# Rotary query halves exchanged by transfers between SBUF places, and the rotary tile copied out by ScalarE

## The reference, cut to what matters

```python
cq = rms_norm(h @ w_dq, q_gain)
q = jnp.einsum('bsr,rhd->bshd', cq, w_uq)          # 16 heads, 128 plain + 64 rotary dimensions
q = jnp.concatenate([q[..., :NOPE_DIM], rope(q[..., NOPE_DIM:], pos)], axis=-1)
q = rms_norm(q, qk_gain_q) * qk_gain_k.astype(q.dtype)

def rope(x, pos):                                   # cos, sin of pos * inv, half = 32
    x1, x2 = x[..., :half], x[..., half:]
    return jnp.concatenate([x1 * cos - x2 * sin, x1 * sin + x2 * cos], axis=-1)
```

## Time and profile before

| what | value |
|---|---|
| runs | 2076.65, 2082.14, 2082.95 us, median 2082.14 |
| the profiled execution | 2079.32 us, span 2077.6 us |
| TensorE busy | 2054.7 us, 99% of the span |
| VectorE busy | 1601.5 us, 77% |
| ScalarE busy | 1104.7 us, 53% |
| GpSimd busy | 342.0 us, 16% |
| granted TensorE clock | 1.000 |

### The profile page before, as it was taken

The page is one execution under the profiler, slowest core; times in us unless marked ns, Lnnn a source line. Parts: engine busy times, 40 slices in busy tenths (PEclk is TensorE's granted clock), DMA queues, the critical chain, the costliest instruction groups (busy, mean ns, idle before and its releaser), DMA issues.

```text
span 2077.6 us, 44241 instructions
## 1 busy us (share of the span) xinstructions
PE 2054.7 (99%) x16692; PEld 1990.6 (96%) x16692; DVE 1601.5 (77%) x2667; ACT 1104.7 (53%) x1898; POOL 342.0 (16%) x384
## 2 busy tenths in 40 slices
PE   9999999999999999999999999999999999999999
PEld 8999999999999999999999999998768889999998
DVE  7779885336367998987999898679665468989987
ACT  6456454443225655655665655545564446656555
POOL 0011111221011111110211111111122121111111
PEclk9999999999999999999999999999999999999999
DMA  5467783322224777775777777441322226777775
GB/s 173 116 165 181 183 194 102 99 84 83 82 82 113 178 183 187 179 183 151 163 184 183 185 174 192 132 122 30 94 72 82 62 62 158 182 187 179 187 177 129
DMA packets 362556, 293.57 MB, mean 141 GB/s; under 512 B 21592, under 2 KB 329093, under 8 KB 362149
## 3 DMA queue, kind: packets, MB, share of 16 engines
q1 hardware_dynamic: 326266, 226.84, 36.4%
q0 software_dynamic: 35824, 64.37, 19.0%
q10 hardware_dynamic: 314, 0.37, 0.1%
HBM read 224.57 MB, written 2.66 MB: 109 GB/s over the span
## 4 chain that ended last, share of the span: by engine, by line
PE 88%; DMA 5%; DVE 4%; issue 2%; ACT 1%; SPq 1%; ACTq 0%; DVEq 0%
PE side L825 28%; PE main L776 26%; PE main L825 20%; PE side L1368 2%; DMA raw<-raw 2%; PE main L1130 2%; DMA sums_w<-raw 1%; PE main L1298 1%; PE side L1338 1%; DVE w_lo L2102 1%; DMA raw<-in_ffn_w_gate 1%; PE side L1220 1%; PE main L1200 1%; PE side L1044 1%; PE main L1377 1%
## 5 line engine op out<-in xcount | busy, mean ns | idle before, releaser
L825 PE MATMUL side<-xw_hi,w_hi 128*128 128x260 f32 x1344 | 380.7, 283 | 6.0 <-ACT main L1543 2.6
L825 PE MATMUL side<-xw_hi,w_lo 128*128 128x260 f32 x1344 | 381.0, 283 | 0.0
L825 PE MATMUL side<-xw_lo,w_hi 128*128 128x260 f32 x1344 | 380.1, 283 | 0.0
L2102 DVE TENSOR_TENSOR w_lo<-raw,w_hi 128x512 fp32r<-128x512 f32 (+2 forms) x472 | 323.3, 685 | 35.1 <-ACT w_hi L1488 15.5
L825 PE MATMUL main<-xw_hi,w_hi 128*128 128x260 f32 x1008 | 286.1, 284 | 0.0
L825 PE MATMUL main<-xw_lo,w_hi 128*128 128x260 f32 x1008 | 284.7, 282 | 0.0
L825 PE MATMUL main<-xw_hi,w_lo 128*128 128x260 f32 x1008 | 284.5, 282 | 0.0
L825 PEld LDWEIGHTS side<-xw_hi,w_hi 128*128 128x128 f32 x1344 | 253.2, 188 | 8.6 <-ACT main L1543 3.5
L825 PEld LDWEIGHTS side<-xw_hi,w_lo 128*128 128x128 f32 x1344 | 253.2, 188 | 0.0
L825 PEld LDWEIGHTS side<-xw_lo,w_hi 128*128 128x128 f32 x1344 | 252.8, 188 | 0.0
L2102 DVE TENSOR_TENSOR w_lo<-sums_w,w_hi 128x1024 fp32r<-128x1024 f32 (+1 forms) x232 | 218.6, 942 | 1.0 <-ACT w_hi L1471 1.0
(11 more groups left out here) (460 smaller groups left out, 5334.4 us busy)
## 6 DMA issues: line engine op xcount, KB each, us to landing
sums_w<-raw POOLq DMA_DIRECT2D x112, 256.0 KB, 3.3
raw<-raw POOLq DMA_DIRECT2D x112, 256.0 KB, 5.1
raw<-in_ffn_w_gate SPq DMA_DIRECT2D x86, 256.0 KB, 4.4
raw<-in_ffn_w_gate SPq DMA_DIRECT2D x43, 512.0 KB, 6.1
raw<-in_ffn_w_up SPq DMA_DIRECT2D x84, 256.0 KB, 4.2
raw<-in_ffn_w_up SPq DMA_DIRECT2D x42, 512.0 KB, 6.1
raw<-in_gmlp_w_in SPq DMA_DIRECT2D x16, 1024.0 KB, 5.5
raw<-in_ffn_w_down SPq DMA_DIRECT2D x56, 256.0 KB, 3.9
```

The source lines that it names most:

```text
L825: mm = nc.tensor.matmul(into[j], w_tiles(w, weights_at(s, j))[:, k, :], moving[:, k, order[j], :], start=(j in (0, 1) and k == 0 and i == ...
L2102: a = nc.vector.tensor_tensor(dst, src, hi.bitcast(F32), ALU.subtract)
```

## The change

The eight products with the constant `swap` are left out. Instead SP issues, for each pair of heads, four transfers from `tq` to a new tile `tq_swapped`, each moving 32 partitions of 2080 bytes to the neighbouring block. The rotary tile is copied out of PSUM by ScalarE, ahead of its square, and no longer by VectorE, and has a semaphore of its own, `tq_copied`; `evac_done` counts plain tiles alone (16 in the stage). VectorE's `rope_b` reads `tq_swapped`, and stands one tile later (at u % 3 == 1); that of the last pair stands behind the copies of the turned rows. In SP's queue the exchange of pair 0 stands between page loads 20 and 21, ahead of chunk 2; that of pair 1 ahead of chunk 3; those of pairs 2 to 7 ahead of the last page loads. `tq_swapped` has one place, so an exchange waits for the `rope_b` before it. The semaphore `c_squared` is replaced by a third count on `cq_squared`.

```diff
--- before.py
+++ after.py
@@ -272,6 +272,7 @@
         cq = sb("cq", [P, 2, TOK], F32, proj)
         trig_g = sb("trig_g", [P, 2, TOK], F32, proj)
         tq = cq
+        tq_swapped = sb("tq_swapped", [P, TOK], F32, proj)
         rope_a = sb("rope_a", [P, TOK], F32, proj)
         rope_b = sb("rope_b", [P, TOK], F32, proj)
         sq_hi = sb("sq_hi", [P, 2, TOK], F32R, proj)
@@ -384,7 +385,7 @@
         factors_set = sem("factors_set")
         cq_squared = sem("cq_squared")
         cqn_set = sem("cqn_set")
-        c_squared = sem("c_squared")
+        tq_copied = sem("tq_copied")
         c_set = sem("c_set")
         kr_swapped = sem("kr_swapped")
         kr_part = sem("kr_part")
@@ -477,9 +478,14 @@
         at_ffn[2] = ffn_past(at_ffn[1])
         at_mla = ffn_past(at_ffn[2])
         at_uq = at_mla.past(chunk=2, tile=4, evac=4, h=2, rms=3)
-        at_wo = at_uq.past(chunk=4, tile=24, evac=24)
+        at_wo = at_uq.past(chunk=4, tile=24, evac=H)
         at_ffn[3] = at_wo.past(chunk=8, tile=16, evac=16, h=H, norm=1, sums=KD, xg=KD, xh=KD)
         at_ffn[3].groups = LAST_GROUPS
+
+        def nope_tiles(u):
+
+            return 2 * (u // 3) + min(u % 3, 1) + 1
+
         P_AT = [0, 1, 3, 6]
         PT_AT = [0, 4, 8, 7]
         at_end = ffn_past(at_ffn[3], last=True)
@@ -692,12 +698,26 @@
                         sp.dma_start(pieces[k][:, j, :], cache_mla[0, bass.ds(page, 1), :, :].rearrange("a p d -> (a p) d"))\
                             .then_inc(nat_in[k // 4], 16)
 
+            def swap_halves(r_):
+
+                sp.wait_ge(tq_copied, r_ + 1)
+                if r_ >= 1:
+                    sp.wait_ge(rope_b_set, r_ + 1)
+                for lo in range(0, P, ROPE // 2):
+                    other = lo ^ ROPE // 2
+                    sp.dma_start(tq_swapped[lo:lo + ROPE // 2, :], tq[other:other + ROPE // 2, r_ % 2, :])\
+                        .then_inc(swapped, 16)
+
             n = at_uq.chunk
             for c in range(4):
                 if c == 2:
                     sp.wait_ge(pages_in, 16)
                     sp.wait_ge(tile_done, at_mla.tile)
-                    load_pages(0, 6)
+                    load_pages(0, 5)
+                    swap_halves(0)
+                    load_pages(5, 6)
+                elif c == 3:
+                    swap_halves(1)
                 sp.wait_ge(lo_done, at_uq.lo + c - 1)
 
                 src = mla_w_uq[0].rearrange("(k p) h d -> k p h d", p=P)[:, :, 4 * c:4 * c + 4, :]
@@ -707,6 +727,8 @@
                         .then_inc(uq_rope_in[c % 2], 16)
                     sp.dma_start(dst[:, 0:4 * NOPE].rearrange("p (h d) -> p h d", h=4), src[k, :, :, 0:NOPE])\
                         .then_inc(uq_rope_in[c % 2] if k else raw_in[c % 2], 16)
+            for r_ in range(2, H // 2):
+                swap_halves(r_)
             sp.wait_ge(tile_done, at_wo.tile)
             sp.wait_ge(lo_done, at_wo.lo)
             load_pages(6, 10)
@@ -1078,7 +1100,7 @@
             pe.wait_ge(lo_done, n + 2)
             out_tile(0, 1, KD, xg_hi, xg_lo, free=e + 1, before={4: latent_sum})
             out_tile(1, 1, KD, xg_hi, xg_lo, free=e + 2)
-            pe.wait_ge(c_squared, 1)
+            pe.wait_ge(cq_squared, 3)
             wide_sum(2, ones, [square[:, 0, :]]).then_inc(rms_mm, 1)
             pe.wait_ge(evac_done, e + 4)
             pe.wait_ge(root_done, at_mla.rms + 2)
@@ -1087,13 +1109,6 @@
 
             n, e = at_uq.lo, at_uq.evac
             pe.wait_ge(h_lo_done, at_uq.h)
-
-            def turn_rope(u):
-
-                r_ = u // 3
-                pe.wait_ge(rope_b_set, r_ + 1)
-                pe.wait_ge(evac_done, e + u + 1)
-                wide_sum(0, swap, [tq[:, r_ % 2, :]]).then_inc(swapped, 1)
 
             def q_norms(u):
 
@@ -1120,7 +1135,12 @@
                 c, part = u // 6, u % 6
                 if part == 0:
                     pe.wait_ge(lo_done, n + c + 1)
-                pe.wait_ge(evac_done, e + u - 1)
+                if u < 2:
+                    pe.wait_ge(evac_done, e + u - 1)
+                elif u % 3 == 1:
+                    pe.wait_ge(tq_copied, u // 3)
+                else:
+                    pe.wait_ge(evac_done, e + nope_tiles(u - 2))
                 h0 = 2 * (part // 3)
                 for k in range(2):
                     for i, (w, moving) in enumerate(((w_hi, h_hi), (w_hi, h_lo), (w_lo, h_hi))):
@@ -1131,11 +1151,8 @@
                                                   moving[:, k, half * HALF:(half + 1) * HALF],
                                                   start=(k == 0 and i == 0), stop=(k == 1 and i == 2))
                 mm.then_inc(tile_done, 1)
-                if u % 3 == 0 and u > 0:
-                    turn_rope(u - 1)
                 if u >= 2:
                     q_norms(u - 2)
-            turn_rope(23)
             q_norms(22)
             q_norms(23)
             for j in range(4):
@@ -1148,8 +1165,9 @@
             mm.then_inc(kn_done, 1)
 
 
-            pe.wait_ge(rope_b_set, 9)
+            pe.wait_ge(rope_b_set, 1)
             pe.wait_ge(evac_done, at_wo.evac)
+            pe.wait_ge(tq_copied, H // 2)
             for b in range(QB + 1):
                 w = P if b < QB else NS
                 if b == 0:
@@ -1911,7 +1929,7 @@
                 act.wait_ge(cqn_set, m + 1)
                 nc.scalar.activation(h_hi[:, m, :], cq[:, m, :], ACT.Copy).then_inc(h_hi_done, 1)
             act.wait_ge(evac_done, e + 3)
-            nc.scalar.activation(square[:, 0, :], c_t[:], ACT.Square).then_inc(c_squared, 1)
+            nc.scalar.activation(square[:, 0, :], c_t[:], ACT.Square).then_inc(cq_squared, 1)
             act.wait_ge(rms_mm, at_mla.rms + 3)
             act.wait_ge(rstd_done, at_mla.rms + 2)
             nc.scalar.activation(halves(root[:, :]), side[:, 2:4, 0:HALF], ACT.Sqrt, scale=1.0 / KL,
@@ -1925,8 +1943,18 @@
                     act.wait_ge(q_ssq, u - 1)
                 elif u >= 2:
                     act.wait_ge(sq_lo_set, 2 * ((u - 2) // 3) + (u - 2) % 3 + 1)
-                act.wait_ge(evac_done, e + u + 1)
-                src = tq[:, u // 3 % 2, :] if part % 3 == 2 else qn[:, 4 * c + 2 * (part // 3) + part % 3, :]
+                if part % 3 == 2:
+                    src = tq[:, u // 3 % 2, :]
+                    if u >= 6:
+                        act.wait_ge(tq_squared, u - 5)
+                        act.wait_ge(rope_a_set, u // 3 - 1)
+                        act.wait_ge(swapped, 64 * (u // 3 - 1))
+                    act.wait_ge(tile_done, t + u + 1)
+                    nc.scalar.activation(halves(src), main[:, u % 2, :, 0:HALF], ACT.Copy).then_inc(tq_copied, 1)
+                    act.wait_ge(tq_copied, u // 3 + 1)
+                else:
+                    act.wait_ge(evac_done, e + nope_tiles(u))
+                    src = qn[:, 4 * c + 2 * (part // 3) + part % 3, :]
                 nc.scalar.activation(square[:, u % 2, :], src, ACT.Square).then_inc(tq_squared, 1)
                 if part % 3 < 2:
                     h = 2 * (u // 3) + part % 3
@@ -2765,14 +2793,13 @@
             nc.vector.tensor_copy(hot_rope[:, P - 1:P + 1], two).then_inc(factors_set, 1)
 
             def rope_b_part(r_):
-                dve.wait_ge(swapped, r_ + 1)
+                dve.wait_ge(swapped, 64 * (r_ + 1))
                 if r_ >= 1:
                     dve.wait_ge(qr_set, r_)
                 else:
                     dve.wait_ge(kr_set, 1)
                     dve.wait_ge(factors_set, 3)
-                nc.vector.tensor_tensor(halves(rope_b[:, :]), side[:, 0:2, 0:HALF], halves(trig_g[:, 1, :]),
-                                        ALU.mult).then_inc(rope_b_set, 1)
+                nc.vector.tensor_tensor(rope_b[:], tq_swapped[:], trig_g[:, 1, :], ALU.mult).then_inc(rope_b_set, 1)
 
             def rope_sum(r_):
                 dve.wait_ge(rope_b_set, r_ + 2)
@@ -2793,12 +2820,10 @@
                     at = kv_third(part - 3)
                     nc.vector.tensor_tensor(w_lo[:, 0, at], wkv_flat[:, at], kv_hi[:, at].bitcast(F32),
                                             ALU.subtract).then_inc(kv_lo_set, 1)
-                if part % 3 == 2 and u >= 6:
-                    dve.wait_ge(tq_squared, u - 5)
-                    dve.wait_ge(rope_a_set, u // 3 - 1)
-                dve.wait_ge(tile_done, t + u + 1)
-                dst = tq[:, u // 3 % 2, :] if part % 3 == 2 else qn[:, 4 * c + 2 * (part // 3) + part % 3, :]
-                nc.vector.tensor_copy(halves(dst), main[:, u % 2, :, 0:HALF]).then_inc(evac_done, 1)
+                if part % 3 < 2:
+                    dve.wait_ge(tile_done, t + u + 1)
+                    nc.vector.tensor_copy(halves(qn[:, 4 * c + 2 * (part // 3) + part % 3, :]),
+                                          main[:, u % 2, :, 0:HALF]).then_inc(evac_done, 1)
                 if part % 3 > 0:
                     h = 2 * (u // 3) + part % 3 - 1
                     dve.wait_ge(sq_hi_set, h + 1)
```

(6 more changed lines are left out.)

## The result

The changed kernel takes 2088.32 us, the median of 9 runs (2083.19 to 2089.44); the kernel before, run beside it, 2078.30 (9 runs, 2074.05 to 2082.95). The ratio is 1.0038, with a 95% interval of 1.0029 to 1.0048: slower, by a little over the 0.3% that I had called the bound of what can be told. Forecast were 2078.5, with a range to 2086.0. A second series of both kernels, later, gave 2082.47 (11 runs) for 2080.36 (21 runs), ratio 1.0014 (1.0005 to 1.0023). The two intervals don't meet, so differences of about 0.2% between series exist that an interval doesn't hold; what both say is: slower, by 0.38% in one series and 0.14% in the other. The profiled execution took 2089.44, its span is 2087.7.

A forecast was written before the change was run, and what follows sets the result against it. TensorE, busy 99%, was taken as the bound, VectorE close behind. Terms -0.8, +0.9, +1.75, +1.0, -0.2 and -0.6 gave about 2 us saved: 2079.3 to 2077.3 profiled, 2078.5 named; range 2072.5 to 2086.

The forecast's parts named there:

- The first chunks: Query-tile stage up to tile 12: ScalarE's copy and SP's queue delay tiles 6 and 12, each 0.8 us behind.
- Four issues at 0.4: SP's queue: ScalarE's tq ready about 1389.5, exchange 0's four issues at 0.4 us end at 1391.1.
- Chunk 2's own four loads: SP's weight loads behind exchange 0 and four page loads: issued by 1397.6 instead of 1392.8.
- The landing: Chunk 2's weights land 3.1 to 3.6 us after issue, about 1400.7; ScalarE wants them at 1399.6.
- Nothing gets through: Rival: chunk 2 another 1 us late, or pages later behind exchange 7, eats the gain; 2079 to 2081; chance 0.12.
- the late landing: Rival: exchanges landing past 3.3 us make rope_b on VectorE wait; at 5.1, 6.9 slower, 2086; chance 0.12.
- Then the gain: Tiles 12 to 23: tile 18 even after a 13.0 us beat, tile 23's end 1.85 ahead, 2.6 at about 1450.
- the seven pieces keep their 4.6: VectorE's chain behind ScalarE's third split, three subtractions, two copies, sq_lo, rope_b, stays 4.6 us, plus some 0.2.
- What SP is late with next: SP's 40 last page loads behind exchange 7 start only 0.15 us earlier, so TensorE meets a wait.
- The cap: At the last pages: slack 1.9 plus 0.15, so at most 2.05 of TensorE's 2.6 us lead gets through.
- the landing 2.0: Exchange transfers on SP land 2.0 us after issue, hidden before rope_b with 1.1 to 1.4 over.
- the end of the stage: After tile 23 the last sum comes 2.4 us later instead of 3.44, without the product: 1.0 gained.

The follow-up runs named there:

- the unused transfers: Kernel before plus eight transfers of 32 by 2080 bytes, used by nobody, issued by SP just ahead of its 40 last page loads; ratio 1.0036.
- chunk 2 first: Changed kernel with chunk 2's four loads moved ahead of exchange 0 and of the four page loads that stood between them; ratio 1.0003.
- exchange 7 out of SP's queue: Changed kernel with chunk 2's loads ahead of exchange 0 and the last pair's exchange made by TensorE's product again; ratio 0.9994.
- VectorE's copies: Changed kernel with the rotary tile copied by VectorE again, the exchange staying with the transfers; ratio 1.0029.
- the transfers alone: Kernel before with the 32 exchange transfers added in the changed kernel's places, their data unread, product and VectorE's copy kept; ratio 1.0031.
- GpSimd's issues: Changed kernel with all exchange transfers issued from GpSimd's queue ahead of its rope_a, SP's order as before the change; ratio 1.0011.
- GpSimd's issues and the split first: Changed kernel with exchanges issued by GpSimd and ScalarE's third weight split put ahead of its rotary-tile copy; ratio 0.9994.

## Why the prediction was wrong

The step that failed is **The first chunks**, in its part on SP: chunk 2 was to land at 18.8 of the stage's time (1400.7 in the forecast's times) with ScalarE standing 1.1. It landed at 21.8 (1405.66) with ScalarE standing 4.30. The 3.0 are three terms of the sum, each taken too low:
- *Four issues at 0.4.* The page loads take 0.34 (L698 in the chain of the changed kernel), and I took a small transfer to be like them. An exchange issue takes 0.51 to 0.64 and the four 2.52, start to end: 0.9 more than my 1.6.
- *Chunk 2's own four loads.* I took 2.1; they took 2.90, since one took 1.32: 0.9 more with a gap ahead of them. A row of this kind, 1.90, was in the earlier trace rows, and I used it only in a rival.
- *The landing.* I took 3.6 from the last issue, the larger of the earlier trace rows; it was 4.88: 1.3 more. Why is open. More traffic isn't to be seen: over the 8 us from chunk 2's issue to its landing the DMA share is 0.64, and over the 7 us in which it landed before, 0.66. The nearest thing in the traces is the next exchange: over all kernels, the last load of a chunk landed 4.2 to 4.9 after its issue in seven of the eight places where an exchange was issued less than 1 us behind it (3.5 in the eighth), and 3.0 to 4.0 in 22 of the 23 places with no exchange near (4.4 in the other). No run tests this alone.

The rival *Nothing gets through* named this mechanism, with 1 us and the time 2079 to 2081. With 3 it eats more than the gain. It had the place and a third of the size. The rival for slower that I had priced, the late landing, was the wrong one: 2.0 held, and it was its place in the queue that was waited for, not the exchange's own time. That this rival's time, 2086, lies near the measured one is luck.

**Then the gain.** The six tiles from 12 to 18 were forecast at 13.0 and came out 13.8. The working was right up to "the seven pieces keep their 4.6": one of them took 0.7 longer because GpSimd's rope_a, which waits for the rotary copy, now starts 0.5 before the subtraction and no longer with it. I had listed what the copy's move does to ScalarE and VectorE, and not to the third engine that waits for it. That rope_a could lengthen a subtraction was in no term of the sum. The last six tiles took their forecast time: from the start of tile 18 to that of tile 23 it is 10.3, before 11.9, forecast 10.2.

**What SP is late with next.** The cap was right in kind and in size (slack 1.9 forecast, 1.8 in the experiment with the unused transfers), the input was not: the pages start at 61.4, not at 55.6. Of the 5.8, 4.2 come with tile 23; the rest are the four issues at 0.6 and the 0.85 between the last of them and the first page. By the cap, 5.65 less 1.9 is 3.75 lost; the first product of the scores is 4.06 later than before. So the pages decide what the two losses together cost. TensorE was late without them too: it came to the page wait 2.6 later than before, and the wait added 1.4. At the first product of the scores, chunk 2 first is worth 4.0 (121.2 after tile 0 becomes 117.2, before 117.1), since it moves tile 23 and the pages behind it, and exchange 7 out of SP's queue another 1.4 (115.7).

**Right were:** the copy's 0.66 (0.59), the landing 2.0, its being hidden in the settled chunks, the end of the stage, the place of the page wait, that ScalarE stands before chunk 2's first split. The Trainium skill's rule that transfers to disjoint halves of the partitions serialize (DMA: Bandwidth & Descriptors, Rules for kernel authors), 8.6 for four by the prediction's estimate, did not show: a landing is 2.0 after its own issue, with issues 0.6 apart, and exchange 0 took 3.97 from its first issue to its last landing. Exchanges 1 and 6 took 2.0 to 3.1 to land. What four transfers cost over one is the issuing; one transfer of 128 partitions wasn't tried.

**What stays open.** From the marks the changed kernel loses 5.6 and 3.7 us in the two profiled executions; the timed losses are 7.9 (0.38%) and 2.9 (0.14%). Of the first 5.6, 1.5 arise between the first scores (4.06 late) and the last mark, at the fallen clock. With VectorE's copies mark and ratio agree, 6.2 and 6.0; with the transfers alone they say 5.5 and 6.5, with the unused transfers 3.3 and 7.5. With GpSimd's issues the mark is 1.0 ahead and the time 2.3 behind.

One part of this is in the timed runs themselves, which have a granted clock each. It was full (1.000) in 52 of 108 runs of the kernel before, and in none of the 20 of the changed kernel, the 12 with VectorE's copies and the 5 with the unused transfers. An estimate of what it takes is the missing share of the mean clock times the run: 1.3 to 1.8 us before, 3.9 and 4.2 for the changed kernel, 4.4 with VectorE's copies, 3.0 with the transfers alone, 2.8 with GpSimd's issues, 5.4 with the unused transfers. For the unused transfers that is 3.9 of the 4.2 that the mark leaves open, and for the transfers alone 1.1 of 1.0. It doesn't settle the changed kernel, whose second series lost as much clock and less time, nor the one with VectorE's copies. The stretch behind the last mark, the same instructions, took 562.2 before and 564.8 in the changed kernel, but over all the profiled executions it lies between 560.8 and 564.8, in no order of the changes. So a part of the timed loss stays without a cause, and leads of 1 to 2.6 at the last mark are at the edge of what the times can show.

## What to carry to other kernels

When work moves from an engine to a transfer, price the issuing queue as an engine: each issue at its own duration there, each wait at what is queued behind it, and then ask which load that is already on its way to being late stands behind it. Here issues of 2.5 us in front of one chunk of weights and of 40 pages cost more than eight products gave back. And when an instruction moves, list everybody who waits for its result, a third engine too: its new start can fall on another's instruction.

## What the runs showed of the hardware

The granted clock of TensorE fell in the changed kernel behind its wait for the page and the pause before the scores. A row of TensorE's timeline in the changed kernel, then windows of it (busy us by engine, then PEclk):

```profile
1505.07 0.33 PE L1301 MATMUL main<-c_hi,q_hi 128*128 128x128 f32 x1 [1.57 <-DVE few L2953]
...
1505.00:1506.00 1.00, 0.93 (x6) 0.93 (x7) 0.45 (x4) 0.45 (x1) 0.00 (x0) 0.84 0.00 0
1506.00:1509.00 3.00, 3.00 (x13) 2.19 (x14) 0.00 (x0) 1.26 (x4) 0.00 (x0) 0.50 0.03 5
1509.00:1510.00 1.00, 1.00 (x8) 0.64 (x8) 0.22 (x1) 0.00 (x0) 0.00 (x0) 0.96 0.00 0
```

That is 0.50, the lower level, 1.2 GHz, for about 3.4 us, which cost some 1.5. Ahead of it TensorE had been idle for 1.24 from 1489.45 on and 1.57 from 1503.50 on. The kernel before has the same 1.57 pause there and no fall. With the transfers alone (a wait of 2.13), and with the unused transfers (3.13), the clock stayed at full speed from the wait to the scores. In the kernel with GpSimd's issues and the split first it fell behind the 1.57 pause with no wait for a page ahead (0.50 in 1500 to 1502), and in the second series of the changed kernel behind the stand for chunk 2 (0.59 in 1404 to 1406, 0.56 in 1406 to 1408, where TensorE had been busy 1.54 of the 4 us before). So a wait was followed by a fall in some executions and not in others, and a fall came without one. The timed runs differ by kernel: the clock was full in 52 of 108 runs before and in none of the 37 of the changed kernel, of the one with VectorE's copies and of the one with the unused transfers, but in 4 of 11 with chunk 2 first, which waits 1.76 for a page, and in 1 of 11 with GpSimd's issues, which doesn't wait for one. What a stall costs can be more than its length; what decides it is open.

The second is the pair of the earlier trace rows and the changed kernel's 1423.64: a VectorE subtraction takes 0.78 or 1.48, and GpSimd's multiplication 1.95 or 1.31, by which of them began first; 0.5 us decide it.
